# Feed-forward layers of a three-block transformer kernel: down projections moved into seven-product units, the second block's gate and up with them, and the last four feature tiles by token halves

## The reference, cut to what matters

```python
def swiglu_ffn(x, w_gu, w_down):            # first block, D_FF = 2816 = 22 * 128
    a, u = jnp.split(x @ w_gu, 2, axis=-1)
    return (jax.nn.silu(a) * u) @ w_down
# layer: x = layer_norm(ALPHA * x + 0.5 * swiglu_ffn(x, ...), g, b)
def swiglu(x, w_gate, w_up, w_down):        # second block, also 2816 features
    return (jax.nn.silu(x @ w_gate) * (x @ w_up)) @ w_down
# layer: h = h + 0.5 * swiglu(rmsnorm(h, g), w_gate, w_up, w_down)
```

## Time and profile before

| | |
|---|---|
| median of 3 runs | 3017.22 us |
| the profiled execution | 3015.58 us |
| its span | 3014.3 us |
| TensorE busy (matmul) | 2961.4 us, 98% |
| VectorE busy | 1835.2 us, 61% |
| ScalarE busy | 1348.4 us, 45% |
| GpSimd busy | 583.4 us, 19% |
| mean of the granted TensorE clock | 0.997 of 2.4 GHz |

### The profile page before, as it was taken

One profiled execution on the slowest core, in us unless ns is written; L12 is line 12 of the kernel. 1 busy time (PEld: TensorE's weight loads), 2 busy tenths in 40 slices (PEclk: granted clock), 3 DMA queues, 4 the chain that ended last, 5 costly groups with the idle time before them and its releaser, 6 DMA issues.

```text
span 3014.3 us, 46624 instructions
## 1 busy us (share of the span) xinstructions
PE 2961.4 (98%) x19086; PEld 2616.7 (87%) x19086; DVE 1835.2 (61%) x2832; ACT 1348.4 (45%) x2332; POOL 583.4 (19%) x495
## 2 busy tenths in 40 slices
PE   9999999999999999999999999999999899999999
PEld 7998877899988999886789988899998768788888
DVE  6884566688746887365598853744323866554432
ACT  5552376455524554266455532522223556542321
POOL 0222143302221123034311131100003222200000
PEclk9999999999999999999999999999999999999999
DMA  4333331133332233332223333233233111133332
GB/s 138 113 101 114 97 98 57 57 96 102 115 103 83 92 106 120 93 112 63 64 71 99 106 118 93 78 91 87 90 89 116 50 35 42 36 105 97 93 90 78
DMA packets 76533, 270.10 MB, mean 90 GB/s; under 512 B 8720, under 2 KB 9008, under 8 KB 76064
## 3 DMA queue, kind: packets, MB, share of 16 engines
q1 hardware_dynamic: 74448, 260.08, 28.4%
q0 software_dynamic: 1872, 7.04, 0.7%
HBM read 264.97 MB, written 2.11 MB: 89 GB/s over the span
## 4 chain that ended last, share of the span: by engine, by line
PE 88%; DVE 8%; ACT 2%; issue 1%; DMA 0%; SPq 0%; POOL 0%; DVEq 0%; ACTq 0%
PE psum L424 17%; PE psum L427 17%; PE psum L430 17%; PE psum L677 8%; PE psum L682 8%; PE psum L680 7%; PE psum L488 4%; PE psum L500 2%; PE psum L447 1%; PE psum L443 1%; PE psum L1208 1%; PE psum L445 1%; PE psum L3356 1%; DVE z_sum L1365 1%; DVE w_lo L811 0%
## 5 line engine op out<-in xcount | busy, mean ns | idle before, releaser
L377 DVE TENSOR_TENSOR w_lo<-w_raw,w_hi 128x1024 fp32r<-128x1024 f32 (+1 forms) x300 | 397.2, 1330 | 646.8 <-ACT w_hi L366 646.7
L366 ACT CAST w_hi<-w_raw 128x1024 fp32r<-128x1024 f32 (+1 forms) x346 | 351.4, 1019 | 685.4 <-PE psum L430 643.2
L424 PE MATMUL psum<-x_hi,w_hi 128*128 128x512 f32 (+1 forms) x1648 | 511.2, 351 | 2.6 <-ACT neg_mean L3427 1.8
L427 PE MATMUL psum<-x_hi,w_lo 128*128 128x512 f32 (+1 forms) x1648 | 493.2, 340 | 0.9 <-DVE w_lo L377 0.9
L430 PE MATMUL psum<-x_lo,w_hi 128*128 128x512 f32 (+1 forms) x1648 | 491.2, 339 | 0.1
L424 PEld LDWEIGHTS psum<-x_hi,w_hi 128*128 128x128 f32 x1648 | 283.1, 188 | 58.4 <-issue 18.4
L427 PEld LDWEIGHTS psum<-x_hi,w_lo 128*128 128x128 f32 x1648 | 282.8, 188 | 37.8 <-issue 4.8
L430 PEld LDWEIGHTS psum<-x_lo,w_hi 128*128 128x128 f32 x1648 | 282.8, 189 | 35.9 <-DVE x_lo L3865 0.8
L424 PE MATMUL psum<-h_hi_ffn,w_hi 128*128 128x512 f32 (+1 forms) x792 | 296.4, 374 | 0.0
L430 PE MATMUL psum<-h_lo_ffn,w_hi 128*128 128x512 f32 (+1 forms) x792 | 292.6, 369 | 0.0
L427 PE MATMUL psum<-h_hi_ffn,w_lo 128*128 128x512 f32 (+1 forms) x792 | 292.6, 369 | 0.0
(11 more groups left out here) (436 smaller groups left out, 6760.2 us busy)
## 6 DMA issues: line engine op xcount, KB each, us to landing
w_raw<-in_ffn_gu SPq DMA_DIRECT2D x176, 512.0 KB, 3.6
w_raw<-in_ffn_down SPq DMA_DIRECT2D x64, 512.0 KB, 3.6
w_raw<-in_w_in SPq DMA_DIRECT2D x44, 512.0 KB, 3.6
w_raw<-in_b_gate SPq DMA_DIRECT2D x44, 512.0 KB, 3.6
w_raw<-in_b_up SPq DMA_DIRECT2D x44, 512.0 KB, 3.6
w_raw<-in_b_down SPq DMA_DIRECT2D x32, 512.0 KB, 3.5
w_raw<-in_ffn_down SPq DMA_DIRECT2D x32, 384.0 KB, 3.2
w_raw<-in_b_in SPq DMA_DIRECT2D x24, 512.0 KB, 3.6
```

The source lines that it names most:

```text
L366: nc.scalar.copy(w_hi[s][:, 0:n], w_raw[r][:, 0:n]).then_inc(*w_high.inc(u))
L377: nc.vector.tensor_tensor(w_lo[s][:, 0:n], w_raw[r][:, 0:n], w_hi[s][:, 0:n].bitcast(F32), ALU.subtract).then_inc(*w_low_dve.inc(u))
L424: nc.tensor.matmul(out, w_h, hi[:, c], start=first and i == 0, stop=False)
L427: nc.tensor.matmul(out, w_l, hi[:, c], start=False, stop=False)
```

## The change

- `COMBINED` now has all six feed-forward parts: b2_ffn1 and b2_ffn2 also do gate and up of `f` 4 to 21 in units, the wide one with products of 264 columns.
- The down projection over hidden tiles 0 to 17 is done in three chunks of six tiles. For each chunk and each pair of output tiles there is a unit of the same seven products with 3 tiles instead of 4 in each (12 units in each part); its results are added to `x`, scaled. Units of both kinds stand in one list, `ffn_units`, and run through the same orders. In a down unit GpSimd adds `x` to the three copies before VectorE's joins (`pool_add`).
- The combinations of the hidden tiles that such a unit needs are made by a new class `Hidden`: for each pair of hidden tiles up to 17, GpSimd forms n1, t3, n2, t4 (256 columns each), ScalarE casts the four together (1024 columns) and GpSimd makes their low part (1024). All low parts of hidden tiles are on GpSimd. `h_hi` and `h_lo` for all 22 tiles give way to a ring of five pairs.
- Where the root comes late, GpSimd makes three multiplications by the root in each gate and up unit (`pool_root`).
- Hidden tiles 18 to 21 (the tail) are done directly with `pe_out`: all 8 output tiles of token half 0, then of half 1. The norms' ends are those of `MixNorm`, or have its form (`FfnEnd`, `FfnNorm`, `RmsEnd`, `BlockNorm`, `Output`).
- `x` is no longer overwritten, and the rebuilding on GpSimd goes. The sum of weights s2 changes sign, and t3 is kept in place of four tiles' half in `x_hi` and `x_lo`.
- The host reorders the down weights (`chunked`, `tail_pairs`); the bytes loaded are the same.

```diff
+COMBINED = {"ffn1_0": 4, "ffn2_0": 4, "ffn1_1": 4, "ffn2_1": 4, "b2_ffn1": 4, "b2_ffn2": 4}
+CHUNKS = ((0, 6), (6, 6), (12, 6))
+TAIL = 18
+TURNED = TAIL // 2
+HELD = 5
+BLOCKS = 7
...
+def ffn_units(f0):
+    grown = lambda first, end: [("g", f) for f in range(first, end)]
+    down = lambda c, *js: [("d", c, j) for j in js]
+    return (grown(f0, 8) + down(0, 0, 1, 2, 3) + grown(8, 14) + down(1, 0, 1, 2, 3)
+            + grown(14, 20) + down(2, 0) + grown(20, FT) + down(2, 1, 2, 3))
...
+        class Hidden:
...
+            def act_turn(self, pair):
+                act.wait_ge(*self.low.at(("t4", pair)))
+                nc.scalar.copy(self.blocks(pair, 3, 4)[0], self.raw[:]).then_inc(
+                    *self.high.inc(("turn", pair)))
...
+            def pool_step(self, f):
+                for made in self.ready[f]:
+                    pool.wait_ge(*made)
+                if f // 2 < TURNED:
+                    for name in ("t3", "n2", "t4") if f % 2 else ("n1",):
+                        self.pool_combine(name, f // 2)
+                pool.wait_ge(*self.high.at(("h", f)))
+                c, hi, lo = self.of(f)
+                nc.gpsimd.tensor_tensor(lo, self.tile(f)[:, c], hi.bitcast(F32),
+                                        ALU.subtract).then_inc(*self.low.inc(("h", f)))
+            def pool_turn(self, pair):
+                pool.wait_ge(*self.high.at(("turn", pair)))
+                hi, lo = self.blocks(pair, 3, 4)
+                nc.gpsimd.tensor_tensor(lo, self.raw[:], hi.bitcast(F32),
+                                        ALU.subtract).then_inc(*self.low.inc(("turn", pair)))
...
+            def act(self, stored):                       # class Combined
+                for i in range(-1, n + 1):
...
+                    if 0 <= i < n:
+                        self.act_high("up", i)
+                        f = self.grown(i - 2)
+                        if f is not None and f % 2 and f // 2 < TURNED:
+                            self.h.act_turn(f // 2)
+                        f = self.grown(i - 1)
+                        if f is not None:
+                            self.h.act_high(f)
+                        self.act_copy("p2", i)
...
+            def pool(self, total):
...
+                n, late = self.n, self.entry.late
+                for i in range(n + 1):
+                    if i and self.down(i - 1):
+                        self.pool_add("p2", i - 1)
+                    elif i and late:
+                        self.pool_root("b", i - 1)
+                    if i < n and self.down(i):
+                        self.pool_add("r", i)
+                    if i and not self.down(i - 1):
+                        if late:
+                            self.pool_root("again", i - 1)
+                        self.pool_second_half(i - 1)
+                    if i < n:
+                        if self.down(i):
+                            self.pool_add("p1", i)
+                        elif late:
+                            self.pool_root("a", i)
+                    f = self.grown(i - 2)
+                    if f is not None and f % 2 and f // 2 < TURNED:
+                        self.h.pool_turn(f // 2)
+                    f = self.grown(i - 1)
+                    if f is not None:
+                        self.h.pool_step(f)
...
+        class FfnEnd:
...
+            def end_pe(self):
+                self.stat_banks = left[6], left[7]
+                for q in range(1, 2 * KT):
+                    self.pe_tail(q)
+                    if q == KT + self.sums_after:
+                        self.pe_sums(0)
```

More of the change, by code:

```diff
@@ L583, in bank_left, with x_ready @@
+            def x_ready(self, m, i=None):
+                j, odd = divmod(m, 2)
+                c = len(CHUNKS) if i is None else self.units[i][1]
+                if c == 0:
+                    return [self.entry.x_done(m)]
+                last = self.at["d", c - 1, j]
+                if odd:
+                    return [self.joined.at(("up_b", last)), self.first_half.at(last)]
+                return [self.joined.at(("gate_b", last))]
             def bank_left(self, b):
-                fs = range(self.f0, FT)
@@ new lines, in dve_low, with dve_sum @@
+            def dve_low(self, name, i):
+                raw, hi, lo = self.block(name, i)
+                dve.wait_ge(*self.high.at((name, i)))
+                nc.vector.tensor_tensor(lo, raw, hi.bitcast(F32), ALU.subtract).then_inc(
+                    *self.low.inc((name, i)))
+            def dve_sum(self, name, i):
+                gate, up = (w_raw[(self.u[i] + j) % RAW_SLOTS] for j in range(2))
+                n, u = self.half_k(i) * P, self.u[i]
+                first, second = slice(0, n), slice(n, 2 * n)
+                s1, s2, s4 = (self.sums[s][:, first] for s in ("s1", "s2", "s4"))
@@ L819, in dve_sum @@
                 if name == "s1":
                     dve.wait_ge(*loaded[(u + 1) % RAW_SLOTS].at(u + 1))
-                    out, one, two = self.sums["s1"], up[:, first], up[:, second]
+                    done = nc.vector.tensor_tensor(s1, up[:, first], up[:, second], ALU.add)
                 elif name == "s3":
-                    dve.wait_ge(*self.summed.at(("s1", f)))
-                    out, one, two = up[:, first], up[:, first], gate[:, first]
+                    dve.wait_ge(*self.summed.at(("s1", i)))
@@ L825, in dve_sum @@
+                    done = nc.vector.tensor_tensor(up[:, first], up[:, first], gate[:, first],
+                                                   ALU.add)
                 elif name == "s2":
                     dve.wait_ge(*loaded[u % RAW_SLOTS].at(u))
-                    dve.wait_ge(*self.summed.at(("s1", f)))
-                    out, one, two = self.sums["s2"], self.sums["s1"], gate[:, first]
-                else:
-                    dve.wait_ge(*self.summed.at(("s2", f)))
-                    out, one, two = self.sums["s4"], self.sums["s2"], gate[:, second]
@@ L978, in held @@
                 if before:
[L979 to L991 removed]
+                    return [freed(before[-1])]
@@ L993, in ffn_pe @@
+                return [w for b in range(2 if wide else 1) for w in left[bank(i) + b]]
+            half = Combined(tag, u0, f0, own, wide, freed, bank, entry, h, silu, leave.scale,
+                            u_tail)
+            leave.u_second, leave.half, leave.h = u_tail, half, h
+            leave.bank = lambda q: half.tail_banks[q % 6]
             def ffn_pe():
```

1910 lines of the change are left out of this document (961 added, 949 removed).

## The result

The changed kernel takes 3281.22 us (median of 4 runs, 3276.33 to 3282.12) against 3017.05 for the kernel before (4 runs, 3015.0 to 3020.1). The ratio is 1.0871, 95% interval 1.0853 to 1.089. The forecast was 3150 us with a range up to 3205: the direction was right, the size was half.

The account below looks back on a forecast made before the run. The prediction took VectorE's loop as the bound, with GpSimd holding it at the shared port. Terms 67 - 17 - 8 + 39 + 47 + 3 + 2 = +133 us on 3015.6 gave 3148.6, as median 3150 us; range 2955 to 3205.

Parts of the forecast that it names:

- VectorE's loop bounds the units, no slack for the change: Seven-product units go at VectorE's pace, 9.96 us against 9.84 of TensorE work; TensorE loses 0.12 us in each.
- GpSimd and VectorE exclude each other: VectorE operations with both inputs in SBUF and GpSimd's go one after the other, with 0.13 us overlap at each change.
- Gate and up units, first block at 11.15 us: First-block units with added GpSimd work: a pair from 19.9 to 22.3 us, 14 units in each of four parts, +67 us.
- Second block's units at 14.2 and 14.45: Root multiplications on GpSimd lengthen b2_ffn2's and b2_ffn1's gate and up units: +47 and +39 us.
- Down units at 8.04 and 8.15 us: Down units, additions' holds included, take 8.04 us for 8.32 (-17 us over five parts), wide 8.15 for 8.79 (-8).
- GpSimd is worse: Rival: combinations wait on the port, backlog runs into down units at 9 us; +60, 3210 us; chance 0.07.
- Ends and the rest: Feed-forward ends like the mixer's +3 us, tail of direct tiles +2; casts and rebuilding of `x` nothing.
- The signs: For: first-block VectorE 85%, GpSimd over 35%, about 750 matmuls in 100 us. Against: 846, or down units of 7.4 us.
- TensorE as the bound: Rival: VectorE's loop only follows TensorE, so all 118 us of saved matmul work come, less 5: 2904 us; chance 0.10.
- The port packs well: Rival: GpSimd's operations fall on joins and waits, first-block units stay at 9.95 us; sum -46, 2971 us; chance 0.17.

Follow-up runs that it names:

- before_pe_small: Kernel before, third matmul of each product in the seven-product units cut to 64 moving columns from 256: 3017.14 us, ratio 1.0.
- e_pe_small: Changed kernel, third matmul of each of a unit's seven products cut to 64 moving columns from 256: 3290.93 us, ratio 1.091.
- m_port: Separate kernel computing none of the reference: phases of 8 operations of 128x512 per engine, alone and together; VectorE and GpSimd together took 13.4 us.
- e_order: Changed kernel, ScalarE's copy p2 ahead of the hidden tile's casts and GpSimd's hidden work behind the additions: 3251.61 us, ratio 1.0779.
- e_hid_small: Changed kernel, for hidden-tile pairs 5 to 8 GpSimd's combinations, turn low and the tiles' own low parts cut to 8 columns: 3187.06 us, ratio 1.0568.
- e_totals: Changed kernel with most hidden-tile work moved from GpSimd to VectorE (3173.8 us), plus three 512-column totals at first-block part ends moved likewise: 3174.07 us.
- e_floor: Changed kernel with most hidden-tile work moved from GpSimd to VectorE (3173.8 us), plus VectorE's low parts gate and later cut to 8 columns: 3000.12 us.
- before_dve: Kernel before, low part of each hidden tile of the seven-product units (512 columns) moved from GpSimd to VectorE: 3053.97 us, ratio 1.0126.

## Why the forecast was right or wrong

- **VectorE's loop bounds the units, no slack for the change**: right. Narrowing a third of the units' matmuls won nothing, neither in the kernel before (before_pe_small) nor in the changed one (e_pe_small); the chain of the changed kernel is 39% VectorE.
- **GpSimd and VectorE exclude each other**: right, and shown alone in m_port. The Trainium skill's rule of an exclusive lock for the whole instruction (SBUF — State Buffer, "Who interferes with whom") is borne out, but for its edges: a held operation began 0.14 us before the holder's end, and 16 operations in turn took 13.4 us for 14.7 alone, 0.08 us of overlap at each.
- **Gate and up units, first block at 11.15 us**: right in the steady stretch (22.6 us a pair for 22.3), wrong in how many. The first two behind each chunk run at 8.9, the third at 9.8, because their GpSimd work is in the chunk or ahead of it. That the time of a pair came out to 0.3 us does not make each hold of the hand-laid order right; no run looks at them one by one. The 18 units took 186.4 us in ffn1_1 for 195.9 forecast, -9.5.
- **Second block's units at 14.2 and 14.45**: right as a size (14.1 and 14.3 in the steady stretch), again for fewer units: 223.1 and 224.1 us for 246.4 and 250.3 forecast, -23 and -26.
- **Down units at 8.04 and 8.15 us: this step failed.** The term was -17 and -8 us; it should have been a loss. (Its own sum is also off: 7.0 us of VectorE's list and holds of 0.55, 0.2 and 0.2 make 7.9 and not 8.04, which is 6 us over the five parts and not what failed.) Eleven intervals of down units took 115.5 us in ffn1_1 for 88.4 forecast, +27, and 124.6 and 126.2 in the second block, +36 each: some +180 us over six parts, less some 90 from the two points above. At a seam an interval holds work of both kinds; counted one interval later, a down unit is 10.0 to 10.1 us in all six parts and gate and up stand 4 to 11 us a part under the forecast, so by either count the down units are the loss. I summed VectorE's list and the additions' holds, and wrote the hidden work into the gate and up units alone. But what GpSimd has to do for the last two tiles of a group runs at the head of its queue in the chunk, and the additions stand behind it: 99 us of waits. Without that queue order the port would still have taken most of it: 88 us of waits less came with 54 us more of busy time and gave 30 us (e_order). With the hidden work beside it narrow, a first-block chunk is 35.4 us for 41.5 (e_hid_small), against 32.2 forecast: two thirds of the miss in a chunk is that work; the other third was not taken apart. I had this as the rival "GpSimd is worse", at 7 in 100 and 9 us a unit; it was 10.0 to 10.4 in the first block, and the whole came out 71 us above that rival's 3210.
- **Ends and the rest**: 2 to 6 us a part over the forecast in the first block, 13 and 6 in the second block's parts, and 9 us in the mixers, 44 us of the miss. Most of the second block's share has a place. In b2_ffn1 the four direct tiles took 72.9 us for 60.3 before, at nearly the same granted clock:

```profile
1892.30:1952.60 60.30, 53.74 (x391) 52.42 (x392) 44.52 (x68) 33.25 (x67) 12.69 (x14) 0.92 0.29 88
2036.60:2109.50 72.90, 56.62 (x398) 53.73 (x397) 58.97 (x92) 37.59 (x77) 25.27 (x25) 0.91 0.18 59
PE psum L449 <- DVE hid L1370: 8.6, 2, 8.1
```

  The first row is of the kernel before, the others of the changed one. VectorE is busy 14 us more: with units in this part it now makes the combinations of `x` and their low parts here (L835, L885, L882: 12 us), and TensorE waits 8.1 us at once for a join that stands behind the first of them. The forecast put that at nothing, without a reason. In b2_ffn2 the direct tiles take their 46 us as before, but VectorE's first sum for the units takes 2.24 us for 0.69 beside GpSimd's turn low, and TensorE stands still for 3.4 us. That these are the causes is read from the trace and not tested. The first-tile totals are not the cause (e_totals); what the first block's 15 us are stays open.
- **The signs**: all those named for the forecast were there, and none of those against it. A window of first-block units:

```profile
700.00:800.00 100.00, 92.52 (x761) 90.84 (x759) 86.57 (x129) 51.90 (x95) 43.82 (x38) 0.98 0.30 91
```

  761 matmuls, VectorE at 87%, GpSimd at 44%, second-block units at 14 us. They tell lock from no lock and say nothing on down units that are too slow; the one sign on down units was for 7.4 us.
- **The rivals**: TensorE as the bound (2904 us) is refuted, and even a VectorE relieved of 2.2 us a unit gives only 3000 (e_floor). "The port packs well" is refuted for the changed kernel, but it is what the kernel before does with its one low part (before_dve).

Shown: that the hidden work costs by its order (30 us, with the earlier copy), its amount (81) and its engine (107), the lock, that TensorE is not the bound. Argued only: the split of a chunk's time between the single operations of GpSimd, and the second block's openings.

## What to carry to other kernels

When work is added to an engine that shares a port with the bounding one, lay its whole queue over the loop, the seams between kinds of units included: a backlog does not vanish where the next kind of unit looks light. Moving such work to the bounding engine can be a gain (107 us here, where some 165 us of held time and 78 us of waits went for 206 us of operations) or a loss (38 us, where nothing went). By these two what decides is how much of it overlaps the bounding engine's SBUF operations or stands in front of what that engine waits for, not how long it takes. A sign that would come out the same with the doubtful term twice as large does not guard that term. Ask of a saving on an engine that is 98% busy whether any engine waits for it; in the unit of rows 4 and 5 none did.

## What the runs showed of the hardware

A VectorE copy with one SBUF input of 512 columns, 421 ns alone, took 1348 ns beside GpSimd's two-input operations: it is held like the others. GpSimd's memset kept its 525 ns beside VectorE and alone; VectorE's took 485 ns beside GpSimd. Taking a quarter of the columns from TensorE's matmuls in the units did not shorten the units and came with a lower granted clock in the changed kernel, 0.943 for 0.977; in the kernel before the same edit left it at 0.995 for 0.997.
